# Half of the tokens' expert gates through a table in DRAM instead of one-hot matmuls, in a two-layer transformer kernel

## The reference, cut to what matters

```python
def hybrid_layer(x, ...):
    ...                                   # two attention mixers, merged and projected
    x = layer_norm(ALPHA * x + mixed)
    return layer_norm(ALPHA * x + peer(x, ...))

def peer(x, w_query, sub_keys, expert_u, expert_v):     # 8 heads, top 16 of 128*128 experts
    s = einsum('thpd,hpnd->thpn', (x @ w_query).reshape(T, 8, 2, 64), sub_keys)
    sv, si = top_k(s, 16)                               # the best 16 of each half
    cand = sv[:, :, 0, :, None] + sv[:, :, 1, None, :]
    cidx = si[:, :, 0, :, None] * 128 + si[:, :, 1, None, :]
    best, pos = top_k(cand.reshape(T, 8, 256), 16)
    eidx = take_along_axis(cidx, pos)
    gate = softmax(best)
    w = gate * gelu(einsum('chkd,cd->chk', expert_u[eidx], x))
    return einsum('chk,chkd->cd', w, expert_v[eidx])
```

## Time and profile before

| what | us |
|---|---|
| median of 3 runs | 2196.19 (2195.25 to 2196.42) |
| the profiled execution, its own time | 2194.99 |
| its span, first to last instruction | 2193.2 |
| PE busy | 2138.6 (98%) |
| DVE busy | 1491.6 (68%) |
| ACT busy | 1157.8 (53%) |
| POOL busy | 181.5 (8%) |

### The profile page before, as it was taken

One profiled execution on the slowest core, in us unless ns is written; L12 is line 12 of the kernel. 1 busy time (PEld: TensorE's weight loads), 2 busy tenths in 40 slices (PEclk: granted clock), 3 DMA queues, 4 the chain that ended last, 5 costly groups with the idle time before them and its releaser, 6 DMA issues.

```text
span 2193.2 us, 40674 instructions
## 1 busy us (share of the span) xinstructions
PE 2138.6 (98%) x14244; PEld 1919.5 (88%) x14244; DVE 1491.6 (68%) x2764; ACT 1157.8 (53%) x1835; POOL 181.5 (8%) x202
## 2 busy tenths in 40 slices
PE   8999999999999999999999999999999999999997
PEld 7987899999997788888788888999999978888886
DVE  6656767777778855555576566777777797555556
ACT  4456445555558745445444464455555596555443
POOL 2100000000007400000020000000000182000000
PEclk9999999999999999999999999999999999999999
DMA  5622445555550155655454234455555502565554
GB/s 196 196 81 87 154 164 182 182 182 182 182 181 29 58 191 192 201 200 201 163 196 170 87 106 152 166 182 182 182 182 182 173 0 100 195 202 191 201 201 134
DMA packets 97595, 350.33 MB, mean 160 GB/s; under 512 B 11312, under 2 KB 11344, under 8 KB 97520
## 3 DMA queue, kind: packets, MB, share of 16 engines
q1 hardware_dynamic: 94320, 338.69, 45.6%
q0 software_dynamic: 3200, 10.66, 1.5%
HBM read 348.26 MB, written 1.05 MB: 159 GB/s over the span
## 4 chain that ended last, share of the span: by engine, by line
PE 86%; DVE 4%; DMA 3%; ACT 2%; issue 2%; POOL 1%; POOLq 0%; DVEq 0%; SPq 0%; ACTq 0%
PE wide L1536 34%; PE acc L1521 14%; PE acc L1522 13%; PE acc L1523 13%; PE acc L2003 4%; DMA raw<-in_front 1%; DMA raw<-in_peer_v 1%; PE tr L1714 1%; POOL hot_i L574 1%; ACT hot_i L844 1%; PE acc L1874 1%; PE acc L1876 1%; PE acc L1875 1%; ACT hi L601 1%; PE wide L1972 1%
## 5 line engine op out<-in xcount | busy, mean ns | idle before, releaser
L601 ACT ACTIVATE hi<-raw 128x1024 fp32r<-128x1024 f32 (+1 forms) x644 | 676.6, 1051 | 540.5 <-DMA raw<-in_peer_v 339.1
L919 DVE TENSOR_TENSOR lo<-raw,hi 128x1024 fp32r<-128x1024 f32 x520 | 636.8, 1225 | 472.8 <-ACT hi L601 471.1
L1521 PE MATMUL acc<-xT_hi,lo 128*128 128x256 f32 x2544 | 725.4, 285 | 4.4 <-DVE kr L1132 2.0
L1522 PE MATMUL acc<-xT_lo,hi 128*128 128x256 f32 x2544 | 721.8, 284 | 0.0
L1523 PE MATMUL acc<-xT_hi,hi 128*128 128x256 f32 x2544 | 721.6, 284 | 0.0
L1521 PEld LDWEIGHTS acc<-xT_hi,lo 128*128 128x128 f32 x2544 | 490.3, 193 | 10.6 <-issue 4.2
L1522 PEld LDWEIGHTS acc<-xT_lo,hi 128*128 128x128 f32 x2544 | 490.4, 193 | 0.1
L1523 PEld LDWEIGHTS acc<-xT_hi,hi 128*128 128x128 f32 x2544 | 490.2, 193 | 0.0
L1536 PE MATMUL wide<-hi,w_lo 128*128 128x512 f32 x1016 | 313.7, 390 | 3.4 <-DVE w_lo L1462 3.3
L1536 PE MATMUL wide<-lo,w_hi 128*128 128x512 f32 x1016 | 312.9, 389 | 0.0
L1536 PE MATMUL wide<-hi,w_hi 128*128 128x512 f32 x1016 | 312.8, 389 | 0.0
(11 more groups left out here) (306 smaller groups left out, 1936.7 us busy)
## 6 DMA issues: line engine op xcount, KB each, us to landing
raw<-in_peer_u SPq DMA_DIRECT2D x256, 512.0 KB, 3.4
raw<-in_peer_v SPq DMA_DIRECT2D x254, 512.0 KB, 3.5
raw<-in_front SPq DMA_DIRECT2D x114, 512.0 KB, 4.0
ln_par<-in_ln POOLq DMA_DIRECT2D x10, 512.0 KB, 5.1
raw<-in_front SPq DMA_DIRECT2D x12, 384.0 KB, 3.0
w<-in_cmp_w POOLq DMA_DIRECT2D x16, 256.0 KB, 4.1
raw<-in_front SPq DMA_DIRECT2D x8, 312.0 KB, 3.4
xs<-in_x SPq DMA_DIRECT2D x2, 512.0 KB, 4.8
```

What stands on the lines that cost most here:

```text
L601: nc.scalar.activation(hi[:, s, :width], raw[:, s, :width], ACT.Identity).then_inc(hi_done, 1)
L919: nc.vector.tensor_tensor(lo[:, s], raw[:, s], hi[:, s].bitcast(F32), ALU.subtract).then_inc(lo_done, 1)
L1521: mm(dst, lo[:, s, c], xh[:, k], start=k == 0, stop=False)
L1522: mm(dst, hi[:, s, c], xl[:, k], start=False, stop=False)
```

## The change

The gates of the first 128 tokens no longer go through the gate stage.

- A table in DRAM for each layer, 128 (i) x 128 (j) x 128 (token) f32, 8.4 MB. POOL fills it with zeros by eight DMAs of 1 MB during the attention.
- After each of the units 0 to 7 ACT takes the exponential of that unit's scores and their sum (`unit_gates_exp`), and DVE, within the next unit, normalises and writes the 16 positions in the table (`spots`). POOL then issues 16 scatters, one for each pick, each of 128 single f32 values, which are added to the table, and waits until all 16 have landed.
- SP loads with every tile of `peer_v` a 128x128 piece of the table (`gt`, 64 KB in rows of 512 bytes that lie 64 KB apart). Before the first tile of `peer_v` it waits for all 128 scatters.
- DVE multiplies the first half of `big` by that piece, tile by tile (`times_gates`), and ACT waits for this before it splits the tile's `big`.
- The gate stage has 32 steps, for the other 128 tokens. `picks` is transposed for these alone.

```diff
+                for c in range(8):
+                    pool.dma_start(table_rows(l)[:, 2048 * c:2048 * c + 2048].rearrange("i (m n) -> i m n", n=512),
+                                   blank[:].unsqueeze(1).broadcast_to([P, 4, 512])).then_inc(table_blank, 16)
...
+                pool.wait_ge(table_blank, (l + 1) * 8 * 16)
+                for u in range(TABLED):
+                    pool.wait_ge(spots_ready, l * TABLED + u + 1)
+                    for k in range(TOPK):
+                        pool.indirect_dma_start(table[l], bass.IndirectOffsetOnAxis(spots[:, u, k:k + 1], 0),
+                                                picks[:, 2, 0, u * TOPK + k:u * TOPK + k + 1], None,
+                                                compute_op=ALU.add).then_inc(table_added, 16)
+                    pool.wait_ge(table_added, l * NTABLE + (u + 1) * TOPK * 16)
...
+            def load_gates(l, c, s):
+                sp.dma_start(gt[:, s], table_rows(l)[:, bass.ds(c * P, P)]).then_inc(gates_loaded[s], 16)
...
-                load(l, t["peer_v"], T_V, EARLY_TURNS)
+                sp.wait_ge(table_added, (l + 1) * NTABLE)
+                sp.wait_ge(best_ready, l + 1)
+                load(l, t["peer_v"], T_V, EARLY_TURNS, 0, True)
...
+                def unit_gates_exp(u):
+                    act.wait_ge(route_step, route_base(l, u + 1))
+                    part = picks[:, 2, 0, u * TOPK:(u + 1) * TOPK]
+                    nc.scalar.activation(part, part, ACT.Exp, accum_out=usum[:, u:u + 1]).then_inc(unit_exp, 1)
...
                 def split_w_hi(i, c, s):
+                    act.wait_ge(gates_applied, l * NKEYS + (i * SLOTS + (c + 1)))
...
+                    u = i - 1
+                    if 0 <= u < TABLED:
+                        tabled = picks[:, 2, 0, u * TOPK:(u + 1) * TOPK]
+                        stages[9].append(lambda: nc.vector.reciprocal(usum[:, u:u + 1], usum[:, u:u + 1]))
+                        stages[10] += [
+                            lambda: nc.vector.tensor_scalar(tabled, tabled, usum[:, u:u + 1], None, ALU.mult),
+                            lambda: nc.vector.scalar_tensor_tensor(
+                                out=expert[:], in0=picks[:, 0, 0, u * TOPK:(u + 1) * TOPK], scalar=128.0,
+                                in1=picks[:, 1, 0, u * TOPK:(u + 1) * TOPK], op0=ALU.mult, op1=ALU.add)]
...
+                def times_gates(i, c, s):
+                    dve.wait_ge(gates_loaded[s], (l * (NKEYS // SLOTS - (s == SLOTS - 1)) + (i + (c // SLOTS + 1))) * 16)
+                    part = big[:, i + c // JB, :NG, c % JB]
+                    nc.vector.tensor_tensor(part, part, gt[:, s].rearrange("p (g t) -> p g t", t=TB),
+                                            ALU.mult).then_inc(gates_applied, 1)
...
                     for e in range(SLOTS):
                         n = T_V + e + AHEAD
+                        times_gates(i, e + AHEAD, n % SLOTS)
                         split_lo(l, (i + n // SLOTS), n % SLOTS)
                         split_w_lo(i, e + AHEAD, n % SLOTS)
```

125 lines of the change are left out of this document (81 added, 44 removed).

## The result

| | before | changed | forecast |
|---|---|---|---|
| median of the runs | 2196.31 us (2195.25 to 2196.54, 4 runs) | 2130.49 us (2129.85 to 2136.56, 4 runs) | 2118 us |
| ratio | 1 | 0.9707 (95%: 0.9689 to 0.9725) | |
| profiled execution | 2194.99, span 2193.2 | 2136.56, span 2134.6 | |

A forecast was written before the change was run, and what follows sets the result against it. PE was taken as the bound, with all four engines in a circle in the gate stage. 2194.99 - 80.0 - 0.8 + 1.1 + 1.0 + 1.0 + 0.3 = 2117.6, so 2118 us; parts' bounds 2104 to 2150, range 2106 to 2215.

The forecast's parts named there:

- Parts 1 and 2: Gate stage: 32 of 64 steps go in two layers, -80.0 us, transposes -0.8; two DVE products ahead of it, +1.1.
- Part 3: V: a 64 KB load and DVE product more per tile cost 0 in the loop, +1.0 at V's start.
- Part 4: Attention: POOL's zero fill of the tables shares the DMA engines with raw loads, +1.0 us; bounds 0 and 4 a layer.
- Start-up: Program's start: two small POOL instructions stand ahead of the constants that ACT waits for, +0.3 us.
- Part 5: U: eight single-unit exponentials a layer on ACT, each with two table loads, and four small DVE instructions cost 0.
- Part 6: U: 128 scatters a layer on POOL at 1.4 us each, 2.4 allowed, done near 525, cost 0.
- A: Rival: scatters on POOL take 3.07 us each, making everything behind SP's wait late, 2290 us; chance 0.14.
- B: Rival: the gates' loads bound V, each costing the DMA engines 2.3 us, 2400 us; chance 0.08.
- C: Rival: in U each scatter stops DVE for 0.55 us, so less gain, 2178 us; chance 0.11.

The follow-up runs named there:

- the run with pieces: Changed kernel with the eight zero-fill pieces issued one by one, each beside one of SyncE's loads of attention's middle part; 2119.02 us, ratio 0.9648.
- the changed kernel's second measurement: The changed kernel again, unchanged, as control for the other runs of its chip; 2128.00 us, ratio 0.9694 to the kernel before.
- the run before it: Changed kernel, first layer's zero fill in pieces through attention's middle part, second layer's from SyncE in the first layer's gate stage; 2121.01 us, ratio 0.9651.

## Why the prediction was right, and where it was off

**Right in sign and kind, 12 us too fast.** It forecast 2118; the runs gave 2130.5 and 2128.0. The range held the time. Of its two bounds for all parts together, 2150 follows from the bounds of the terms, but 2104 does not: with 82 us for the steps and nothing for the fill and the start of V the sum is 2114.

**Parts 1 and 2, the steps that go and the products ahead of the stage: right.** The gate stages fell by 41.1 and 40.6 us, -81.7 together, where -79.7 was forecast with the products and transposes. 32 steps at the step's own 1.22 to 1.276 us was the right way to cost it, since all four engines are in that circle. The two products cost about 0.7 us a layer, as their reduction to 4 values a row shows (40.57 to 39.86), near the 0.57 forecast. So the steps alone gave some 83 us, 1 beyond their bound of 82. The four transposes lie in U, where the 0.8 us that they should have saved don't show (+0.1).

**Part 3, V: the loop nearly right, its end and one tile of it not costed.** The tile's slack carried the gates: their loads land after 4.1 us, raw tiles 0.9 us later than before, DVE waits 105 us for gates over the kernel, and taking that out leaves the median where it was. The start of V, for which the forecast had +1.0, cost nothing. But V lost 8.0 us in one profile and 4.8 in the other, and the forecast had asked for a PE without waits there. In the first profile 2.9 of the 8.0 us are the two waits of 1.46 us behind the 52nd tile, where a load of the layer norm's rows stands beside those of the weights and the gates. 3.0 are longer waits for the last few tiles, of which the own tile's are 1.0: its product puts DVE, ACT and DVE in series with PE waiting. 1.7 are the stretch at the lower clock behind the own tile's wait. Neither place is in the sum. The run with the own tile's product moved took 6.3 us less, of which the edit itself explains up to 5.4.

**Part 4, the zeros: the term that was wrong,** +1.0 forecast, +12.9 measured alone. This is the largest part of what is missing: in the two profiles of the changed kernel the fronts are 13.6 and 8.1 us over the forecast, of 19.0 and 9.5 in all. The working took the fill as 25 us of DMA time beside loads "far apart" with 2 us of slack, with a bound of 4 us a layer. It did not ask what a load that comes late holds up. The load took 9 us instead of 3.5, which is over that slack; then ACT, in order, held a copy that PE needed; then PE ran at its lower clock. Bandwidth was there, as the run with pieces shows. An upper bound from the queue, 8 MB ahead of one tile on the same 16 engines, would have been 25 us a layer less the slack, and not 4.

**Start-up: small, and above the forecast.** PE's first product comes at 7.2 us in all profiles of the changed kernel and its variants, 6.4 before, where +0.3 was forecast. At the first transposes of the rotated heads (`tr<-ident,rot`, at 108.5 before) they are 0.2 to 2.6 us later, 1.2 in the mean.

**Part 5, table loads: right.** From 22 us after its start to its end, neither U has PE idle time of over 0.3 us.

**Part 6, the scatters: hidden as forecast, by less than it seemed, and with a wrong deadline.** A scatter takes 1.78 us where 1.4 was taken, and with 0.30 us to the next and the waits for landings 2.25 us, so POOL was done at 626 and not near 525. The allowed 2.4 was reckoned to SP's load of `peer_v`. The real deadline is POOL's own `first_i` about 37 us after the present end, so 2.25 + 37/128 = 2.5 us a scatter. Both runs with more scatters agree with it.

**Rivals.** What A foresaw, POOL late and everything behind it late too, is real: with 25% more scatters it takes back 62 of 68 us. It was 0.3 us a scatter away. The 3.07 us for a scatter with two waiting operands was not seen; what stretches some scatters from 1.54 to 2.61 us stays open. Behind A stood the Trainium skill, "SBUF — State Buffer", section "A bandwidth-pool intuition that's wrong (but worth ruling out)", with 3.1 us for a GpSimd DMA beside a VectorE copy; no scatter of the changed kernel took that (1.54 to 2.61 us), and POOL's plain loads in V took 0.56 to 0.62. B is refuted: V's DMA share went from 57% to 67%. C is refuted: the low parts in U beside the scatters took what they always did, while one DVE instruction stretched by half beside POOL's sums of squares. It did so only where POOL's had begun first (0.3 and 0.9 us ahead of it). In the kernel before DVE's began first, by 0.1 us, and took its usual time. Changed kernel, low parts from 342 to 640 and the line in question (count, ns min/median/max), then the same line before:

```profile
L975 DVE TENSOR_TENSOR lo<-raw,hi x104: 1200/1226/1266, 341.4 to 637.9; 128x1024 fp32r<-128x1024 f32 x104
...
L1133 DVE TENSOR_TENSOR rot<-rope_a,rope_b x4: 1083/1358/1631, 53.4 to 1121.1; 128x896 f32<-128x896 f32 x4
```

```profile
L1077 DVE TENSOR_TENSOR rot<-rope_a,rope_b x4: 1082/1084/1084, 52.5 to 1150.3; 128x896 f32<-128x896 f32 x4
```

The Trainium skill, "SBUF — State Buffer", section "Who interferes with whom", has VectorE and GpSimd lock each other out where both read SBUF in that way. The second line agrees with it for POOL's arithmetic; the first shows that a scatter issued by POOL is not such an instruction.

**What stays open:** why two variants, the later layer norm's load and the two scatters more, measured 6.5 and 6.8 us over the changed kernel's second measurement (4.1 and 4.3 over its first); why V's end sometimes has a stretch at the lower clock and sometimes not; and part of the gain of the best version, since its interval meets that of the run before it. The best version, with pieces in layer 0, the gate stage's fill for layer 1 and the early product, takes 2114.7 us: 13.3 less than the changed kernel (whose interval it doesn't meet), and 0.9629 (0.9614 to 0.9643) of the kernel before.

## What to carry to other kernels

A burst of background DMA is costed by the one load that lands late behind it, by what stands in order behind that load's consumer, and by PE's clock after the wait; not by the mean share of the DMA engines. Issue it in pieces, each behind the wait that the kernel's own loads use, or in a stage that loads nothing. Work put on a hidden engine needs its deadline read from that engine's own next instruction, and a small step added to every tile should be looked at where it is last, since there nothing runs beside it, and where another load already stands beside the tile's own.

## What the runs showed of the hardware

- An indirect DMA that adds 128 single values into DRAM takes 1.54 to 2.61 us on POOL, 1.78 in the mean of 256, and 2.25 us in a series of 128 with waits for the landing of each 16.
- In U the DMA share went from 0.54 to 0.71 at 182 GB/s both. Over 162 us, 16 engines and 75 scatters of 128 values that is 0.17 x 162 x 16 / 9600 = 0.046 us of one engine for a value; the forecast had allowed 0.15.
- POOL's scatters take nothing from DVE (1226 ns for a low part, as before) or PE (U of 373.3 and 372.6 us, 372.9 before).
- Eight stores of 1 MB issued back to back land after 16.4 us in the median, and a load of 512 KB issued behind them takes 9.0 us instead of 3.5. Issued one by one, a store lands after 6.9 us.
- The clock: behind PE's wait of 4.8 us in the front it was 0.72 of full speed over 12 us. Behind waits of about 2 us at V's end it was 0.67 over 4 us, in 7 cases of 18.
- With more scatters and a wait of 23 us the clock was at 0.62 in the wait and 0.58 in the 7 us behind it:

```profile
669.00:693.00 24.00, 0.96 (x8) 0.79 (x8) 3.65 (x4) 3.98 (x6) 16.93 (x13) 0.62 0.44 99
693.00:700.00 7.00, 7.00 (x35) 6.64 (x36) 5.00 (x9) 5.41 (x10) 4.15 (x5) 0.58 0.00 0
```
